# Two attention pipelines joined into one, and the block compression stacked over 128 partitions behind the by-token projection

## What is computed

```python
q_nsa, kv_nsa, g_nsa, qkv_sb, g_merge = split(h @ w_in)
kc = gelu(flat(k_cmp blocks + pe) @ w1 + b1) @ w2      # 31 blocks of 32 positions, stride 16; vc likewise
p_cmp = softmax(q @ kc.T * scale, masked) * mask;  o_cmp = p_cmp @ vc
o_slc, o_win = causal softmax attention (8 blocks of 64 chosen out of 8; a window of 512)
o_nsa = g[0]*o_cmp + g[1]*o_slc + g[2]*o_win
# stick-breaking attention, 8 heads of 64:
z = q @ k.T * scale;  log_1m = where(strict, -softplus(z), 0)
w = where(strict, exp(log_sigmoid(z) + cumsum_from_right(log_1m) - log_1m), 0);  o_sb = w @ v
y = sigmoid(g_a)*(o_nsa @ w_proj_nsa) + sigmoid(g_b)*(o_sb @ w_proj_sb);  out = y @ w_out
```

## Time and profile before

| | |
|---|---|
| median of 3 runs | 2919.11 us (2918.11 to 2919.73) |
| profiled execution | 2919.7 us, span 2917.9 us |
| TensorE matmul | 2896.5 us, 99% |
| weight load | 2393.0 us, 82% |
| VectorE | 1815.5 us, 62% |
| ScalarE | 1269.8 us, 44% |
| GpSimd | 183.1 us, 6% |
| granted TensorE clock, mean | 0.998 |

### The profile page before, as it was taken

One profiled execution on the slowest core, in us unless ns is written; L12 is line 12 of the kernel. 1 busy time (PEld: TensorE's weight loads), 2 busy tenths in 40 slices (PEclk: granted clock), 3 DMA queues, 4 the chain that ended last, 5 costly groups with the idle time before them and its releaser, 6 DMA issues.

```text
span 2917.9 us, 38219 instructions
## 1 busy us (share of the span) xinstructions
PE 2896.5 (99%) x14870; PEld 2393.0 (82%) x14870; DVE 1815.5 (62%) x3143; ACT 1269.8 (44%) x2344; POOL 183.1 (6%) x124
## 2 busy tenths in 40 slices
PE   9999999999999999999999999999999999999998
PEld 8788888888888888888887788888888877888886
DVE  5666775345555387733666767775365777677743
ACT  4544443333333354432356644544233765444431
POOL 1000000010000000000100301000030022010000
PEclk9999999999999999999999999999999999999999
DMA  4232323222222232232421132332233112323322
GB/s 154 80 102 94 101 94 101 94 87 80 80 86 80 95 100 94 94 101 86 144 66 37 55 104 81 101 101 95 95 107 115 44 44 73 108 74 101 100 94 73
DMA packets 74725, 263.88 MB, mean 90 GB/s; under 512 B 9008, under 2 KB 9008, under 8 KB 74416
## 3 DMA queue, kind: packets, MB, share of 16 engines
q1 hardware_dynamic: 73680, 258.03, 27.5%
q10 hardware_dynamic: 864, 3.41, 0.3%
HBM read 255.64 MB, written 2.10 MB: 88 GB/s over the span
## 4 chain that ended last, share of the span: by engine, by line
PE 92%; DVE 4%; ACT 3%; issue 1%; POOL 1%; DMA 0%; DVEq 0%; SPq 0%; ACTq 0%
PE bank L546 26%; PE bank L549 25%; PE bank L553 25%; PE bank L623 2%; PE bank L624 2%; PE bank L627 2%; PE bank L755 2%; PE bank L734 2%; PE bank L719 1%; DVE tmp L1657 1%; PE bank L925 1%; DVE wl L1516 1%; DVE big L2201 1%; ACT big L1495 1%; PE bank L710 1%
## 5 line engine op out<-in xcount | busy, mean ns | idle before, releaser
L1516 DVE TENSOR_TENSOR wl<-ring,wh 128x512 fp32r<-128x512 f32 (+1 forms) x928 | 639.7, 696 | 807.8 <-ACT wh L1062 802.8
L546 PE MATMUL bank<-xh,wh 128*128 128x512 f32 x2392 | 944.7, 395 | 0.3 <-ACT wh L1062 0.2
L549 PE MATMUL bank<-xh,wl 128*128 128x512 f32 x2392 | 932.9, 390 | 0.2 <-DVE wl L1516 0.2
L553 PE MATMUL bank<-xl,wh 128*128 128x512 f32 x2392 | 904.7, 390 | 0.0
L1062 ACT ACTIVATE wh<-ring 128x512 fp32r<-128x512 f32 (+1 forms) x928 | 568.9, 622 | 687.5 <-PE bank L553 613.9
L546 PEld LDWEIGHTS bank<-xh,wh 128*128 128x128 f32 x2392 | 449.8, 188 | 105.1 <-issue 12.8
L553 PEld LDWEIGHTS bank<-xl,wh 128*128 128x128 f32 x2392 | 449.7, 188 | 95.0
L549 PEld LDWEIGHTS bank<-xh,wl 128*128 128x128 f32 x2392 | 450.1, 188 | 90.5 <-DVE wl L1516 1.1
L546 PE MATMUL bank<-bigr,wh 128*128 128x512 f32 x1024 | 398.9, 390 | 0.2
L549 PE MATMUL bank<-bigr,wl 128*128 128x512 f32 x1024 | 398.4, 389 | 0.0
L553 PE MATMUL bank<-bigr,wh 128*128 128x512 f32 x1024 | 393.4, 389 | 0.0
(11 more groups left out here) (236 smaller groups left out, 2883.7 us busy)
## 6 DMA issues: line engine op xcount, KB each, us to landing
ring<-in_w_up SPq DMA_DIRECT2D x176, 512.0 KB, 3.5
ring<-in_w_down SPq DMA_DIRECT2D x88, 512.0 KB, 3.5
ring<-in_w_in SPq DMA_DIRECT2D x64, 512.0 KB, 3.6
ring<-in_w_ret SPq DMA_DIRECT2D x32, 512.0 KB, 3.6
ring<-in_w_even SPq DMA_DIRECT2D x19, 512.0 KB, 4.3
ring<-in_w_ret_v SPq DMA_DIRECT2D x16, 512.0 KB, 3.6
ring<-in_w_ret_out SPq DMA_DIRECT2D x16, 512.0 KB, 3.7
ring<-in_w_proj SPq DMA_DIRECT2D x16, 512.0 KB, 3.5
```

Source lines behind the costliest of these rows:

```text
L546: e.matmul(o, K.wh(p, c * 128, 128), oh, start=start, stop=False, skip_group_check=True)
L549: e.matmul(o, K.wl(p, c * 128, 128), oh, start=False, stop=False, skip_group_check=True)
L553: m = e.matmul(o, K.wh(p, c * 128, 128), ol, start=False, stop=stop, skip_group_check=True)
L1516: e.tensor_tensor(K.wl(i, 0, w), K.raw(i), K.wh(i, 0, w).bitcast(F32), ALU.subtract).then_inc(F.lo.tell(("piece", i)), 1)
```

## The change

- The softmax steps and the stick-breaking steps become one list of 32 steps in one `soft` pipeline (`late_steps`), with one filling plan, `fill_late`: 9/4 filling steps per softmax step, 6 per stick-breaking step (as 7, 7, 4), and 11 at the end. The functions `stick` of ScalarE and VectorE go into `soft`. The first half of the split for "y" moves into the pipeline's last turn.
- The compression contracts over 128 partitions: two neighbouring positions of one head are stacked, so that there are 8 positions in place of 16, both heads are in the columns (64 in place of 32), and keys and values stand in the two column halves of one bank. The weights are two raw units in place of four.
- The stacked inputs `K.SK` and `K.SV` are made by eight new SBUF-to-SBUF DMAs per layer on SP (`stack`): those of the values (`vals`) behind turn 2, those of the keys (`keys`) behind turn 4.
- The raw units and the compression move behind "tm"; turns 0 to 4 are now tied to the units of "tm" and the raw units, at the same distance from tile 7's unit as before. `compressed` moves behind sb tile 0, the compressed scores behind sb tile 1, their softmax on VectorE and ScalarE into three lumps behind sb tiles 0, 1 and 2.
- On VectorE the operations of the compressed softmax are those of before, put into functions (`values_low`, `compressed_scores`, `gate_values`, `compressed_probs`), and the low parts of two sb pieces that stood between them are left to the loop over the sb tiles.
- The order of VectorE from tile 7 to the first low parts of "tm" is as it was.

```diff
...
     for l in range(2):
         u = W.stationary(D[f"w_in{l}"], 0, [("n", l, "g")], 40)
         u = W.stationary(D[f"w_in{l}"], u, [("n", l, j) for j in range(5, 8)], DT)
-        for i in range(4):
-            W.raw(D[f"w1_{l}"][i], ("w1", l, i))
         W.moving(D[f"w_tm{l}"], 0, ("tm", l), 280, 3)
+        for part in range(2):
+            W.raw(D[f"w1_{l}"][part], ("w1", l, part))
...
+    K.SK, K.SV = K.big(11424, 1088), K.big(12512, 1088)
+    K.skr, K.svr = (t.rearrange("p (v n r) -> p v n r", v=2, r=16) for t in (K.SK, K.SV))
+    K.hid, K.hb, K.gates = K.big(20640, 128), K.big(20768, 128), K.big(20896, 96)
...
-def fill_nsa(t):
-    return 2 * (t + 1) + (t + 1) // 2
-
-
-def fill_stick(t):
-    return fill_nsa(22) + (4 + 67 * (t + 1) // 15 if t >= 0 else 0)
-
+def fill_late(t):
+
+    after = t - 19
+    if after <= 0:
+        return 9 * (t + 1) // 4
+    return 45 + 18 * (min(after, 12) // 3) + (0, 7, 14)[min(after, 12) % 3] + (0, 4, 7, 11)[max(after - 12, 0)]
...
+    def stack(l, src, dst, flag, name):
+
+        for kv in range(2):
+            for odd in range(2):
+                e.dma_start(dst[64 * odd:64 * odd + 64, 544 * kv:544 * kv + 544 - odd],
+                            src[64 * kv:64 * kv + 64, odd:544]).then_inc(
+                    flag.tell(*([(name, l)] if kv and odd else []), by=16), 16)
+
+    def keys(l):
+        q.wait_ge(F.dve, ("pe", l))
+        q.wait_ge(F.dve, ("rope", l, 0))
+        stack(l, K.KC, K.SK, F.keys, "keys")
+
+    def vals(l):
+        q.wait_ge(F.dve, ("pe", l))
+        q.wait_ge(F.dve, ("freed", "n", l, "g", 1))
+        stack(l, K.VCB, K.SV, F.vals, "vals")
+
     turns = {}
     for l in range(2):
-        u = W.raws["w1", l, 0]
-        turns.update({u + 1: (l, (0, 1)), u + 2: (l, (2,)), u + 3: (l, (3,)), u + 4: (l, (4,)), u + 7: (l, (5, 6))})
+        u = W.raws["w1", l, 0] - 3
+        turns.update({u + 1: (l, (0, 1)), u + 2: (l, (2,)), u + 3: (l, (3,)), u + 4: (l, (4,)), u + 5: (l, (5, 6))})
     for u, (src, width, pieces) in enumerate(W.units):
         if u in turns:
             for r in turns[u][1]:
                 half_turn(turns[u][0], r)
+            if turns[u][1] == (2,):
+                vals(turns[u][0])
+            if turns[u][1] == (4,):
+                keys(turns[u][0])
...
-        for i in range(2):
-            c = (K.kcr, K.vcr)[i]
-            if i == 0:
-                q.wait_ge(F.dve, ("rope", l, 0))
-            else:
-                q.wait_ge(F.dve, ("freed", "n", l, "g", 1))
-            q.wait_ge(F.dve, ("pe", l))
-            b = K.place["cb", l, i] = spare[i]
-            empty(b)
-            for part in range(2):
-                u = W.raws["w1", l, 2 * i + part]
-                q.wait_ge(K.landed(u), ("unit", u))
-                for n in range(16):
-                    for kv in range(2):
-                        r = slice(64 * kv, 64 * kv + 64)
-                        m = e.matmul(BK[b][r, 32 * part:32 * part + 32], K.slot(u)[r, n * 64:(n + 1) * 64],
-                                     c[r, 2 * part:2 * part + 32, n], start=part == 0 and n == 0, stop=n == 15,
-                                     skip_group_check=True)
-                m.then_inc(F.attn.tell(("cmp", l, i, part), ("unit", u)), 1)
-            vacated[b] = [(F.act, ("hb", l, i))]
...
+        by_token(("tm", l), 280, s, F.act)
+        b = K.place["cb", l] = 4
+        q.wait_ge(F.vals, ("vals", l))
+        q.wait_ge(F.keys, ("keys", l))
+        empty(b)
+        for part in range(2):
+            u = W.raws["w1", l, part]
+            q.wait_ge(K.landed(u), ("unit", u))
+            for n in range(8):
+                for i, c in enumerate((K.skr, K.svr)):
+                    at_w = 512 * i + 64 * n
+                    m = e.matmul(BK[b][64 * i:64 * i + 64, 64 * part:64 * part + 64], K.slot(u)[:, at_w:at_w + 64],
+                                 c[:, :, 2 * part:2 * part + 32, 2 * n], start=part == 0 and n == 0, stop=n == 7,
+                                 skip_group_check=True)
+            m.then_inc(F.attn.tell(("cmp", l, part), ("unit", u)), 1)
+        vacated[b] = [(F.act, ("hb", l))]
+
+        def compressed_scores():
+            q.wait_ge(F.act, ("kcc", l))
+            for g in range(4):
+                b = g // 2
+                q.wait_ge(F.dve, ("rope", l, 1 + g))
+                if g % 2 == 0:
+                    empty(b)
+                for i in range(NQ):
+                    c0 = (g % 2 * 4 + i) * 64
+                    m = e.matmul(BK[b][:, c0:c0 + 64], K.NQT[g][:, i * 128:(i + 1) * 128], K.kcc, start=True, stop=True,
+                                 skip_group_check=True)
+                if g % 2:
+                    m.then_inc(F.attn.tell(("cmps", l, b)), 1)
+                    vacated[b] = [(F.dve, ("cs", l, b))]
+
         for j in range(8):
             tile(("sb", l, j), DT, xn(s), F.dve)
+            if j == 0:
+                compressed()
+            if j == 1:
+                compressed_scores()
         by_token(("sbv", l), 512, s, F.act)
 
         fill = fills(steps(("gm", l, j), DT, xn(s), F.dve) for j in range(16))
         half[0] = ("kcc", l)
-        soft(("n", l), nsa_steps(K, l), fill, fill_nsa)
-        soft(("s", l), stick_steps(K, l), fill, fill_stick)
+        soft(("n", l), late_steps(K, l), fill, fill_late)
...
-        by_token(("tm", l), 280, lambda i: K.TM[:, i * 280:(i + 1) * 280], s, None, {3: compressed})
+        by_token(("tm", l), 280, lambda i: K.TM[:, i * 280:(i + 1) * 280], s)
         hi_to(W.first["sb", l, 0] + 3)
-        q.wait_ge(F.act, ("freed", "tm", l, 3))
-        e.activation(K.gv, K.tmq[:, :, 256:280], ACT.Exp, bias=0.0, scale=-1.0).then_inc(F.act.tell(("gexp", l)), 1)
-        q.wait_ge(F.dve, ("csub", l))
-        c2d = bc(K.CS, [[32, 32], [1, 31]])
-        e.activation(c2d, c2d, ACT.Exp, bias=0.0, scale=1.0).then_inc(F.act.tell(("cexp", l)), 1)
+        e.preload_act_table_set("gelu_apprx_tanh_and_others")
+        q.wait_ge(F.attn, ("cmp", l, 1))
+        e.activation(K.hb, K.bank(("cb", l))[:, 0:128], ACT.Copy, bias=0.0, scale=1.0).then_inc(F.act.tell(("hb", l)), 1)
+        q.wait_ge(F.dve, ("hid", l))
+        e.activation(bc(K.hid[:, 64:128], [[32, 2], [1, 31]]), bc(K.hid, [[32, 2], [1, 31]]), ACT.Gelu_apprx_tanh,
+                     bias=K.SM[:, 160:161], scale=1.0).then_inc(F.act.tell(("gel", l)), 1)
+
+        def compressed_exps():
+            q.wait_ge(F.act, ("freed", "tm", l, 3))
+            e.activation(K.gv, K.tmq[:, :, 256:280], ACT.Exp, bias=0.0, scale=-1.0).then_inc(F.act.tell(("gexp", l)), 1)
+            q.wait_ge(F.dve, ("csub", l))
+            c2d = bc(K.CS, [[32, 32], [1, 31]])
+            e.activation(c2d, c2d, ACT.Exp, bias=0.0, scale=1.0).then_inc(F.act.tell(("cexp", l)), 1)
+
         for j in range(8):
             hi_for(("sb", l, j))
+            if j == 0:
+                compressed()
+            if j == 2:
+                compressed_exps()
...
+        def merge():
+            q.wait_ge(F.proj, ("tile", "gm", l, 15))
+            split(("y", l), [(K.NQT[j], F.act, ("on", l, j)) for j in range(4)], 0)
+
         e.preload_act_table_set("natural_log_exp_and_others")
-        stick(("s", l), stick_steps(K, l), lambda t: merge_to(fill_stick(t)))
-        q.wait_ge(F.proj, ("tile", "gm", l, 15))
-        split(("y", l), [(K.NQT[j], F.act, ("on", l, j)) for j in range(4)], 0)
-        q.wait_ge(F.attn, ("values", ("s", l), 11))
-        e.activation(K.SBQ[3], BK[4][:, :], ACT.Copy, bias=0.0, scale=1.0).then_inc(F.act.tell(("os", l, 3)), 1)
...
         rope(4)
-        for i in range(2):
-            hb, bias = K.hb(i), K.SM[:, 160 + i:161 + i]
-            q.wait_ge(F.act, ("hb", l, i))
-            e.tensor_tensor(bias, hb[:, 0:1], hb[:, 63:64], ALU.add).then_inc(F.dve.tell(("hbias", l, i)), 1)
-            q.wait_ge(F.dve, ("hbias", l, i))
-            e.tensor_tensor(bias, bias, K.vec("b1", 2 * l + i), ALU.add).then_inc(F.dve.tell(("hbias1", l, i)), 1)
-            e.tensor_tensor(K.hid[:, 32 * i:32 * i + 31], hb[:, 1:32], hb[:, 32:63], ALU.add).then_inc(
-                F.dve.tell(("hid", l, i)), 1)
         e.memset(K.kcc, 0.0)
...
         lo_to(p + 3)
+        hb, bias = K.hb, K.SM[:, 160:161]
+        q.wait_ge(F.act, ("hb", l))
+        e.tensor_tensor(bias, hb[:, 0:1], hb[:, 95:96], ALU.add).then_inc(F.dve.tell(("hbias", l)), 1)
+        e.tensor_tensor(bc(K.hid, [[32, 2], [1, 31]]), bc(hb[:, 1:128], [[32, 2], [1, 31]]), bc(hb[:, 64:128], [[32, 2], [1, 31]]),
+                        ALU.add)
+        q.wait_ge(F.dve, ("hbias", l))
+        e.tensor_tensor(bias, bias, K.vec("b1", l), ALU.add).then_inc(F.dve.tell(("hid", l)), 1)
         rope(5)
         rope(6)
...
+            if j == 0:
+                values_low()
+            if j == 1:
+                compressed_scores()
+                gate_values()
+            if j == 2:
+                compressed_probs()
...
```

(78 more changed lines are left out.)

233 lines of the change are left out of this document (66 added, 167 removed).

## The result

The changed kernel takes 2927.3 us (median of 8 runs, 2926.4 to 2928.4) against 2918.2 us before (8 runs, 2917.3 to 2919.7): a ratio of 1.0032, 95% interval 1.0023 to 1.0040. It is slower by 9.1 us. The forecast was 2922.9 us with a range of 2913 to 2931: the time lies in the range, 4.4 us above the forecast, and above the 2924.9 us up to which the forecast called it "same". "Same" had a chance of 0.51, "slower" one of 0.35.

The account below looks back on a forecast made before the run. TensorE, busy 99% of the span, was taken as the bound. To 2919.7 us it added 11.4 + 5.7 - 7.6 + 3.2 - 8.1 - 0.8 = +3.8, giving 2923.5, less 0.6 for the median: 2922.9 us, range 2913 to 2931.

Parts of the forecast that it names:

- waits of the by-token projection: First by-token piece: TensorE waits for its low part on VectorE, 6.3 us in layer 0, 5.1 in layer 1.
- clock behind them: After each late layer's standstill before the by-token projection, TensorE's clock falls: 2.9 us per layer, 5.7 in all.
- compression: Compression matmuls in each late layer: 64 records at 60 ns take 3.8 us instead of 7.59, saving 7.6 in all.
- wait of sb tile 4: TensorE waits 1.6 us per layer for a low part queued behind VectorE's compressed probabilities, 3.2 in both layers.
- pipeline: stick waits and visits: Attention steps: stick-breaking waits go, 8.1 us, and two fewer visits to the filling tiles per layer save 0.8.
- The rivals of 30 and 117 ns: Compression matmuls: 30 ns per record gives 2919.1 us (chance 0.08); 117 ns, no saving, gives 2930.5 (chance 0.09).
- The price of the four issues: SP's queue before turn 3: four DMAs stacking the values cost 4 x 0.60 = 2.4 us, range 0 to 4.8.
- have no wait now and about 1.5 us to spare: Softmax steps can give up fill, 2.25 instead of 2.5 per step, to the stick steps at no cost.
- The rival on the slow side: Stick-breaking steps: VectorE's reading of scores stays queued behind scans, so 8.1 us are not won: 2931.0 us, chance 0.14.
- a clock that stays up: By-token projection: the standstill causes no clock fall, 2917.2 us; shares chance 0.24 with hidden stacking.
- stacking that hides: SP's stacking DMAs overlap and cost nothing; with no clock fall too, 2912.4 us; shares chance 0.24.

Follow-up runs that it names:

- both orders mended: Changed kernel with VectorE's by-token low parts ahead of ropes 3 and 4, and two low parts inside the compressed probabilities: 2904.9 us, ratio 0.9956.
- the pipeline alone: Kernel before with only the single softmax and stick-breaking pipeline and its new fill, compression as it was: 2913.0 us, ratio 0.9984.
- without the giving back: Kernel before with only the single pipeline, but 2.5 fill steps per softmax step and 17 per three stick steps: 2909.5 us, ratio 0.9970.
- the first kernel with a fill: Changed kernel with 30 purposeless matmuls between last stationary tile and by-token projection of each late layer: 2929.2 us, ratio 1.0036.
- the second fill: Changed kernel with the same 30 purposeless matmuls ahead of the by-token projection, written to a long-empty bank: 2922.6 us, ratio 1.0017.

## Why the forecast was off, by its own steps

| step | forecast | measured |
|---|---|---|
| waits of the by-token projection | +11.4 (6.6 to 16.2) | +14.9 |
| clock behind them | +5.7 (0 to 5.7) | +5.0 |
| compression | -7.6 | -7.7 |
| wait of sb tile 4 | +3.2 (0 to 5.2) | +3.4 to +4.1 |
| pipeline: stick waits and visits | -8.9 | -5.4 |
| sum | +3.8 | +8.4 by the spans |

The measured terms add up to 10.2 us (with the smaller value for sb tile 4). With the stretch ahead of layer 0 (-1.4) and the small matmuls of the compressed values (0.92 us per layer before and 0.48 now, so -0.9 in all) the sum is 7.9 of the 8.4 us.

**The compression** was right: 64 records in 3.75 us (start of line 1010 to what follows), 59 ns each, by the row of the value matmuls with the same weight shape. The rivals of 30 and 117 ns are out. The second was the rule of the Trainium skill (TensorE: Matmul & The Clock Gate, Part 3) that a weight load overlaps only with matmuls of another row group: for weights of 128 rows in alternating column halves the trace disagrees. Over these 3.75 us the weight loads are busy for 3.58 us and the matmuls for all of it, with one row group throughout. The runs agree: both orders mended is 8.2 us below the pipeline alone.

**The waits of the projection** had the right place and a wrong size, and the parts can be read off. Counted from TensorE's arrival, in layer 0: rope 3's multiply comes at +1.2 us, where the forecast had +2.5 (0.06 in the earlier trace rows, and 2.4 for SP); the multiply of rope 4 follows 3.96 us later, where it had 3.14; TensorE is released 2.17 us after that, where it had 1.05. In layer 1: +1.7 against +1.25, 4.53 against 3.14, and 2.18 against 1.05, by these rows:

```profile
2179.28 0.69 DVE L2048 TENSOR_TENSOR pp<-pp,rope 128x512 f32<-128x512 f32 x1 [3.66 <-DMA pp<-tmp]
...
2183.81 0.69 DVE L2048 TENSOR_TENSOR pp<-pp,rope 128x512 f32<-128x512 f32 x1 [1.33 <-DMA pp<-tmp]
2184.42 2.23 DVE L1506 TENSOR_TENSOR wl<-ring,wh 128x280 fp32r<-128x280 f32 x3
```

That layer 0 came near the forecast (7.1 us of waiting against 6.3) is in part luck: rope 3 came 1.3 us earlier than forecast, the two steps behind it took 0.8 and 1.1 us longer. Between SP's last issue of turn 3 and rope 3's multiply there were 3.3 us before (1391.87 to 1395.17) and are 1.4 us now (1393.45 to 1394.88), so of the 3.0 us by which the issue comes later against TensorE's arrival only 1.2 reach VectorE. Why the transfer is quicker no run separates.

Two terms were missing. First, rope 4's turn is queued on SP behind the same four DMAs as rope 3's. The forecast shifted rope 3 and kept the distance to rope 4 as in the earlier trace rows, where VectorE did not wait for turn 4 at all. Now it does, 0.75 and 1.33 us. Second, GpSimd's multiply: 1.1 us in each layer. In the kernel before, the low parts waited 2.26 us for ScalarE and started at 1401.25, when GpSimd's multiply (1398.29, 1.83 us) had ended, so nothing was held up. The price of the four issues was right, 2.52 us against 2.4. SP's timeline in layer 0, and then turn 3 in layer 1:

```profile
1385.36 2.41 SPq L479 DMA_DIRECT2D pp<-tmp  x4
1387.82 2.52 SPq L486 DMA_DIRECT2D big<-big  x4
1390.49 0.47 SPq L523 DMA_DIRECT2D ring<-in_w_tm  x1
1391.00 2.45 SPq L479 DMA_DIRECT2D pp<-tmp  x4
...
2174.10 3.75 SPq L479 DMA_DIRECT2D pp<-tmp  x4
```

In layer 1 the four issues of turn 3 take 3.75 us instead of the 2.41 of the earlier trace rows, and rope 3 comes 2.9 us later against TensorE's arrival than before, not 2.4. With the values stacked later turn 3 takes 2.41 us there, and turn 4, which then follows closest, 3.30. What holds SP up for a microsecond in layer 1 and not in layer 0 stays open; no run separated it.

**The clock** was right in its mechanism and near in its size: 2.5 instead of 2.9 us per layer. The row that gave the price, a fall early in the program, is itself not the same in every trace (last section).

**The wait of sb tile 4** was right in place, cause and size: 1.72 us against 1.6.

**The pipeline** is the step whose reasoning failed. The stick waits went as forecast: without the giving back it is 4.6 us per layer against 4.5. Wrong was the sentence that the softmax steps could pay for the fill because they "have no wait now and about 1.5 us to spare"; no row stands behind the 1.5 us. With 6 instead of 9 fill matmuls ahead of its transposes, ScalarE falls behind and 1.9 us per layer come back in pieces too small for the view of waits. The rival on the slow side, that the bank wait would stay, is not what happened.

The waits of the projection and the pipeline are each 3.5 us worse than forecast, together more than the 4.6 us by which the spans miss the sum. The clock's term (0.7), the stretch ahead of layer 0 (1.4) and the small matmuls (0.9) gave most of the rest back. The last two were in no term of the forecast: that the time came within 4.4 us owes something to them.

Of the rivals, a clock that stays up, stacking that hides and a bank wait that stays did not occur.

## What to carry to other kernels

When work that fills TensorE's time is moved away from a place, list what VectorE still owes at that place and put it into the idle time that VectorE has just before, ahead of its waits for transfers: here that was worth 18 us. When a DMA is put into a queue, shift every transfer behind it, not only the next one, and look whether a VectorE operation with both inputs in SBUF now falls together with one of GpSimd. That no wait shows at one fill rate does not prove that there is slack for a lower one: when the rate is lowered, compare how long the same group of matmuls takes up to the start of what follows, not the waits.

## What the runs showed of the hardware

A VectorE operation with two inputs in SBUF that started 0.3 to 0.5 us behind a GpSimd multiply of 1.5 to 1.7 us stood until that ended (1.51 us for an operation of 0.44); one that started 0.1 us ahead of it was not slowed. The twelve traces hold 68 such operations that started behind a GpSimd multiply of a rope and before its end; those of 280 columns ended 0.3 us after the multiply and those of 512 columns 0.55 us after it, whenever they had started. The 24 that read one input from a bank took 0.68 to 0.69 us as always. The multiply itself took 1.26 to 1.29 us with VectorE idle, and mostly 1.70 to 1.77 us where VectorE had started 0.1 us ahead of it.

After every standstill of TensorE between 4.4 and 8.5 us (counted from start to start), eight in four of the kernels, 13 to 25 matmuls ran slowly, the first one behind it counted: up to 0.40 us for that one, 0.233 us instead of 0.127 for the others. The standstills of 6.4 and 6.7 us had 13, the one of 4.4 us 16. A ninth, of 4.7 us in the first kernel with a fill, had 12 matmuls of 512 columns at 0.427 us instead of 0.227. The waits of 1.7 us in the earlier trace rows and of 0.8 us behind the second fill had none.

The fall of the clock early in the program, which the forecast took as its price, is not fixed. The same 24 tiny matmuls stand there in every kernel, and the mean clock from 33 to 42 us was 0.63 before, 0.81 in the changed kernel, and 1.00, no fall at all, in the kernel with both orders mended. The three rows:

```profile
33.00:42.00 9.00, 9.00 (x29) 0.63 0.17 58
```

```profile
33.00:42.00 9.00, 9.00 (x41) 0.81 0.18 58
```

```profile
33.00:42.00 9.00, 9.00 (x47) 1.00 0.19 58
```

From the start of these 24 matmuls to the next such group it is 11.45 us before (30.64 to 42.09) and 9.86 after (30.88 to 40.74); with the 0.24 us by which the second starts later this is the 1.4 us of the table's first row. In the ten traces without a fill the last stationary tile of layer 0 ends between 1391.9 (both orders mended) and 1395.1 us (before). There is one trace of each kernel, so whether this goes with the kernel or changes from one execution to the next is not shown; a comparison of two single profiles can have 3 us of it.
